# Four constant products behind the routing are given up in a two-layer decoder trunk with a mixture of experts

## What is computed

```python
def hierarchical_moe(hn, w_group, b_group, w_router, b_router, w_gate, w_up, w_down):
    """Top-1 expert group, then top-2 experts inside it; gate = p_group * softmax(top-2 logits)."""
    t = hn.reshape(-1, d)
    g_logits = (t @ w_group + b_group).astype(F32)
    g_idx = jnp.argmax(g_logits, axis=-1)
    e_logits = (t @ w_router + b_router).astype(F32).reshape(-1, N_GROUPS, EXPERTS_PER_GROUP)
    e_sel = jnp.take_along_axis(e_logits, g_idx[:, None, None], axis=1)[:, 0]
    top_v, top_i = lax.top_k(e_sel, EXPERT_TOPK)
    ...
    for grp in range(N_GROUPS):
        a = jnp.einsum("nd,edf->nef", t, w_gate[grp])
        u = jnp.einsum("nd,edf->nef", t, w_up[grp])
        act = jax.nn.silu(a) * u * gates[:, grp, :, None]
        y = y + jnp.einsum("nef,efd->nd", act, w_down[grp])
```

## Time and profile before

| | us |
|---|---|
| median of 3 runs | 1024.01 |
| lowest and highest | 1022.69 and 1026.19 |
| the profiled execution | 1024.96 |
| its span | 1023.1 |
| TensorE busy, share of the span | 963.0, 94% |
| VectorE (DVE) busy | 459.1, 45% |
| ScalarE (ACT) busy | 238.7, 23% |
| moved by DMA | 275.73 MB, mean 269 GB/s |

### The profile page before, as it was taken

How to read it: one execution, slowest core, us unless ns; L and a number is a source line. 1 busy time by engine, 2 the same in 40 slices (tenths; PEclk the granted TensorE clock), 3 DMA queues, 4 the chain that set the end, 5 groups by cost and what they waited for, 6 DMA issues and landing times.

```text
span 1023.1 us, 13905 instructions
## 1 busy us (share of the span) xinstructions
PE 963.0 (94%) x5576; PEld 651.8 (64%) x5576; DVE 459.1 (45%) x1159; ACT 238.7 (23%) x590; POOL 184.3 (18%) x136
## 2 busy tenths in 40 slices
PE   7999999999989899999899999999998999998986
PEld 5888688868556666665444877446855766665542
DVE  5644722386463332222236538677546232222215
ACT  3223700272221000000013226456121100000102
POOL 5640172006001111112102201001401011111100
PEclk9999999999999999999999999999999999999999
DMA  9639502155768999999999220145286999999996
GB/s 334 222 130 207 160 11 102 55 206 172 294 240 299 416 420 419 420 419 420 418 341 289 83 82 2 35 187 209 80 356 214 365 420 419 420 420 418 420 392 266
DMA packets 66594, 275.73 MB, mean 269 GB/s; under 512 B 16019, under 2 KB 20611, under 8 KB 41946
## 3 DMA queue, kind: packets, MB, share of 16 engines
q1 hardware_dynamic: 56528, 257.48, 65.1%
q0 software_dynamic: 10000, 17.34, 4.9%
HBM read 260.64 MB, written 30.44 MB: 284 GB/s over the span
## 4 chain that ended last, share of the span: by engine, by line
PE 70%; DMA 18%; DVE 6%; issue 3%; SPq 1%; POOL 1%; ACT 1%; DVEq 0%; POOLq 0%
PE bank L991 16%; PE bank L1263 12%; DMA K<-rows,small 10%; PE bank L1040 6%; PE bank L1104 6%; PE bank L1277 5%; PE bank L1113 5%; PE bank L1058 3%; DMA hnT<-in_moe_w_down 3%; DMA W<-in_moe_w_up 3%; PE bank L1074 2%; PE bank L1462 2%; PE bank L1174 1%; DMA D<-expert_rows 1%; PE bank L1252 1%
## 5 line engine op out<-in xcount | busy, mean ns | idle before, releaser
L2137 DVE SCALAR_TENSOR_TENSOR PT<-bank,small,PT 128x256 f32<-128x256 f32 x32 | 15.5, 484 | 203.9 <-PE bank L1263 203.9
L1277 PE MATMUL bank<-D,PT 128*64 128x512 f32 x416 | 101.6, 593 | 5.5 <-DMA D<-in_moe_w_down 3.3
L772 POOL DMA_INDIRECT expert_rows<-K,small x30 | 30.3, 1009 | 342.2 <-DVE K L2159 316.9
L2159 DVE SCALAR_TENSOR_TENSOR K<-K,small,bank 128x512 f32<-128x512 f32 x64 | 47.8, 747 | 87.6 <-PE bank L1277 87.4
L1263 PE MATMUL bank<-W,PT 128*64 128x256 f32 x640 | 78.1, 385 | 8.7 <-DMA W<-in_moe_w_up 5.5
L1263 PE MATMUL bank<-W,cst 128*64 128x256 f32 x640 | 77.8, 383 | 0.0
L1670 ACT ACTIVATE P<-P,nm 128x128 f32<-128x128 f32 (+5 forms) x128 | 68.3, 536 | 22.1 <-DVE nm L1916 21.7
L1710 ACT ACTIVATE PT<-bank 128x256 f32<-128x256 f32 x32 | 12.3, 383 | 260.6 <-PE bank L1269 243.6
L1040 PE MATMUL bank<-K,Q 128*128 128x256 f32 (+3 forms) x256 | 70.5, 417 | 1.4 <-DVE nm L1916 1.0
L1263 PEld LDWEIGHTS bank<-W,PT 128*64 128x64 f32 x640 | 50.0, 137 | 31.6 <-issue 10.3
L1277 PEld LDWEIGHTS bank<-D,PT 128*64 128x64 f32 x416 | 36.1, 137 | 49.4 <-issue 44.5
(11 more groups left out here) (317 smaller groups left out, 1804.1 us busy)
## 6 DMA issues: line engine op xcount, KB each, us to landing
D<-in_moe_w_down SPq DMA_DIRECT2D x48, 1024.0 KB
W<-in_moe_w_gate SPq DMA_DIRECT2D x40, 1024.0 KB
W<-in_moe_w_up SPq DMA_DIRECT2D x36, 1024.0 KB
hnT<-in_moe_w_down SPq DMA_DIRECT2D x12, 1024.0 KB
W<-in_e_w_in SPq DMA_DIRECT2D x5, 2048.0 KB
expert_rows<-K SPq DMA_DIRECT2D x2, 4096.0 KB, 37.1
V<-in_moe_w_gate SPq DMA_DIRECT2D x6, 1024.0 KB
Q<-in_moe_w_gate SPq DMA_DIRECT2D x6, 1024.0 KB
```

Source lines behind the costliest of these rows:

```text
L1277: last = nc.tensor.matmul(bank[5 + half][at, :], hT[:, 128 * c + 64 * a:128 * c + 64 * a + 64], d[:, col:col + 512], start=(c == 0), stop= ...
L2159: nc.vector.scalar_tensor_tensor(rows[:, at], rows[:, at], own[:, p:p + 1], bank[5 + half][:, :], ALU.mult, ALU.add).then_inc(s_ye, 1)
```

## The change

The call at the end of `mixer_out` goes, in both layers, since both run the same function. The two other calls of `stay_busy` remain.

```diff
                 for c in range(C):
                     last = nc.tensor.matmul(bank[7][:, 128:160], ones, ohs[:, c, :], start=(c == 0), stop=(c == C - 1))
                 last.then_inc(s_ws, 1)
-                stay_busy(4, 512)
```

## The result

| | before | changed |
|---|---|---|
| median, us | 1024.11 | 1026.76 |
| lowest to highest, us (22 runs each) | 1022.6 to 1027.97 | 1024.78 to 1031.82 |
| the profiled execution, us | 1024.96 | 1029.12 |
| its span, us | 1023.1 | 1027.2 |

The kernel is slower: by 2.65 us going by the two medians, and by 3.1 us going by the ratio, which is 1.003 with a 95% interval of 1.0021 to 1.0039 (2.2 to 4.0 us) and is not the quotient of the medians. Ratios in this document leave out executions far longer than the others of their kernel; there are two, of 2018.68 and 4711.88 us, both of the kernel with layer 0 alone changed, and no trace shows a reason for them. The profiled execution of the changed kernel is one of its longer ones, 2.4 us above its median.

The account below looks back on a forecast made before the run. TensorE is busy 94% of the span, but expert weights' DMA sets the pace in the expert stages. A net loss of 1.4 us a layer, 2.8 us for both, on the 1024.01 us median gave 1026.8 us; range 1023.0 to 1029.8 us.

Parts of the forecast that it names:

- The bound and the delay's way to the end: Expert stages: weights set the pace; a later first group of gates moves their whole stream and the end.
- one for one: From the first pair's gates to the end: a later start shifts the weight stream by the same time.
- hardly anything being loaded: Between routing and experts: DMA share 0.00 at 307 to 308 us and 0.31 at 316 to 318 us.
- The removed queue: Products ahead of the first transposes: removal gains 0.43 us in layer 0, 0.7 in layer 1, 1.1 together.
- The chain's 10.39 us: Constant products' links in both layers; rival that their whole sum falls away, giving 1013.6 us; chance 0.02.
- The clock: After a 4.6 us TensorE pause, the granted clock is at half over the transposes, first gates, or both.
- one slow stretch of some 3.4 us: Over the first gates in each layer: a single slow stretch, +2.2 to +3.4 us in all; chance 0.55.
- 1.4 was taken and 1.1 to 1.7 given as ends: Net loss per layer at the first gates: 1.4 us, between 1.1 (early start kept) and 1.68 (eaten).
- The transposes at half speed: Second four transposes in layer 0: 0.45 us of chain takes up to 0.9, eating the 0.43 us earlier start.
- The clock back before the gates: Rival: full clock again before the first gates, only transposes pay; −1.1 to +0.5 us, about 1023.7 us; chance 0.22.
- Two slow stretches: Rival: second stretch over the first pair, gates over 6 us; +3.4 to +5.8 us, about 1028.8 us; chance 0.17.

Follow-up runs that it names:

- more products (8): Kernel before with five constant products in place of four, and one more 512 wide between the third slots and last ranks; 1024.70 us, ratio 1.0013.
- layer 1 changed (4): Kernel before with the four constant products given up in layer 1 alone; 1025.17 us, ratio 1.0018.
- layer 0 changed (3): Kernel before with the four constant products given up in layer 0 alone; 1026.3 us, ratio 1.0017.
- narrow products (2): Kernel before with its four constant products 32 columns wide in place of 512, in both layers; 1026.04 us, ratio 1.0019.
- two products (7): Kernel before with two constant products in place of four, in both layers; 1026.62 us, ratio 1.0022.
- eight products (1): Kernel before with eight constant products in place of four, in both layers; 1029.82 us, ratio 1.005.
- runs 5 and 6: Second profiled executions, nothing edited: 5 of the changed kernel, 1026.90 us; 6 of the kernel before, 1022.09 us.

## Why the prediction was right

**The bound and the delay's way to the end.** The fronts of all ten profiles, with the time of the profiled execution:

| kernel | front, layer 0 | layer 1 | sum | time, us |
|---|---|---|---|---|
| before, second profile | 9.81 | 9.84 | 19.65 | 1022.09 |
| more products (8) | 10.05 | 9.83 | 19.88 | 1024.43 |
| before | 10.53 | 10.57 | 21.10 | 1024.96 |
| layer 1 changed (4) | 9.87 | 11.58 | 21.45 | 1024.60 |
| layer 0 changed (3) | 12.11 | 9.86 | 21.97 | 1026.39 |
| narrow products (2) | 10.89 | 11.26 | 22.15 | 1024.50 |
| two products (7) | 11.39 | 11.23 | 22.62 | 1027.31 |
| changed, second profile | 12.02 | 11.34 | 23.36 | 1026.90 |
| changed | 12.50 | 11.72 | 24.22 | 1029.12 |
| eight products (1) | 12.30 | 14.00 | 26.30 | 1031.65 |

They come from three jobs, whose medians of before are 1024.11, 1023.98 and 1023.42 us. A straight line through them rises by 1.3 us for one us of front (give or take 0.15), with 0.8 us of scatter about it. That the end follows the front is shown; whether exactly one for one, as the prediction had it, is not, since single executions scatter by as much. In the first profile of the changed kernel the front of layer 0 is 1.97 us longer, and layer 1 comes 1.32 us later (784.84 against 783.52, from a start 0.30 us earlier). At SP's first load of gates in layer 1 it is 2.47 us behind, and 4.1 us at the end of the span. The last 1.6 us came in the expert stage of layer 1. One link of the chain there, the downs of a pair at 928.42, took 6.60 us at half clock, where 3.67 us stood at 924.52 in before; whether that comes of the change was not settled. One reading of the prediction is too strong: hardly anything being loaded holds for the two stretches that it shows, and between them, from 308 to 316 us, before's table has DMA shares of 0.38 to 0.87 (the gathers and SP's half tile). The loads that reuse the first pair's buffers wait for its gates all the same: in the changed kernel the share is down to 0.06 from 316.6 to 318, just ahead of the gate loads.

**The removed queue.** Its price of 0.43 us in layer 0 was read too low. The idle 0.24 us before the weight load at 310.88 does not confirm the landing: the loads of the constant products at 310.02 and 310.45 have the same 0.24 us before them, with `issue`, so this load came in the rhythm of the queue and the rows could have been there before. Without a queue the transposes' weight loads of layer 0 began 3.60 to 3.89 us after the gather's issue (runs 5 and 6 and the profile after), which from 306.87 gives 310.5 to 310.8. The two profiles of before put the queue's price at 0.72 us in layer 0 (10.53 − 9.81) and 0.73 us in layer 1, where 0.7 was right. And it belongs to one execution: in the second one the products were done before the rows came, and there was no queue. The chain's 10.39 us were, as said, no gain; the link that took their place is the gather, 3.85 us.

**The clock.** It fell as forecast, in all eight fronts of the profiles in which the products were given up or narrowed. The term that was mis-sized is the length of it: the prediction took one slow stretch of some 3.4 us. Read in steps of 0.1 us, the clock was at half for 3.5 us in each front of before's first profile, and in the six fronts without products for 10.3, 7.0, 6.9, 6.9, 10.3 and 6.9 us. The first part fell into the pause, and 4.1 to 6.1 us were left for the transposes and the gates, more than the 3.4 us that were priced. The loss is nevertheless close. The mean front of the six without products is 11.88 us (12.50, 11.72, 12.02, 11.34, 12.11, 11.58), that of the six with the four at their place 10.08 us (10.53, 10.57, 9.81, 9.84, 9.86, 9.87): 1.8 us a layer, where 1.4 was taken and 1.1 to 1.7 given as ends. Twice that is 3.6 us, inside the measured 2.2 to 4.0. Against the two fronts that the prediction read (10.53 and 10.57) it is 1.3 us, against the four in which the products were done in time 2.0 us. So the mechanism was right, and that the number is so near is in part luck: 1.4 us was the middle of two ends and came from no row, and the longer slow time is offset in part, since some of it ran beside DVE's copy, for which TensorE waited 0.43 us in before.

**The transposes at half speed,** which no row of before showed, take 1.97 us in place of 1.05 to 1.16; and in layer 0 the gates began only when the last one was done, 1.99 us after the first (310.46 to 312.45), where it was 1.47 us (311.31 to 312.78). That is 0.5 us for the slow transposes, against the 0.45 that was put down, and it ate the earlier start of 0.55 us almost whole. The rest of the 1.97 us is the gates.

**The rivals.** The clock back before the gates: not seen in any of the six fronts, the nearest is the 10.89 us with narrow products. Two slow stretches: in length this rival was nearer than the forecast, since the clock stayed at half for 6.9 us and more, and the transposes alone did not bring it back. Its price was not reached, because the first of that time lay in the pause: from the first gate to SP's load it took 4.7 to 5.7 us, against 3.7 in before and the over 6 that it named.

The same work meets the slow clock in one execution and not in the next: in before, the four products of layer 0 took 5.33 us in one profile and 3.68 in the other, and the fronts of either kernel differed by 0.4 to 0.7 us. The Trainium skill ("TensorE: Matmul & The Clock Gate", section "What's actually happening") says that the count of slow matmuls differs from run to run; these profiles agree. By its section "HAM oscillation — how this bites in real kernels", half of the slow time in which the engine works is lost; from 310.46 to 316.5 at half clock that would be an estimate of 3.0 us. The trace agrees, with 1.97 + 5.67 us where 1.05 + 3.67 stood, 2.9 us, but part of it ran beside DVE's copy, and the front is 1.97 us longer. What the prediction took from that section, that matmuls behind a wait for a DMA start at half rate, is so in the eight fronts with no or narrow products, where the transposes took 1.97 us, and not with two products, where behind a pause of 2.5 us they still took 1.16 and 1.24 us.

## What to carry to other kernels

A matmul that feeds nothing can be worth its place, if it fills a wait in front of work that decides when a stream of loads begins; judge it by the clock over the work behind it and not by its own length in the chain of waits. In this kernel it had to last nearly until that wait ends: four products cover it, two came out as bad as none within the intervals, and eight delay the work themselves. Filling ahead of a short dependent step can hold that step up, as the added product of run 8 did with the ranks in one layer.

## What the runs showed that was not expected

The clock may fall after the pause is over: with two products it was at full speed in a pause of 2.5 us and over the transposes that followed, and was low only behind them (0.81 in 312.3 to 314, 0.54 in 314 to 317). Behind the long pause it then stayed at half two to three times as long as in before (6.9 to 10.3 us against 3.5). And two executions of the unchanged kernel differed by 1.45 us in the sum of their fronts and by 2.9 us in time, 0.7 us of which lies between the medians of their jobs (1024.11 and 1023.42).
